# Hybrid decoder layer: host-made channel-first arrays for x, p, weights and vectors, and a per-layer-embedding gate computed channel by channel

## The reference

```
u = rmsnorm(x) * ln_mix;  [x_lru | g_lru | q | k | v] = u @ w_in            # 1024 x 2560
y_lru = rglru(causal_dwconv4(x_lru), gates, lam) * gelu(g_lru)
y_att = moba(rmsnorm(q) * q_gain, rmsnorm(k) * k_gain, v)                   # 2 key blocks of 256, ALiBi
h = x + concat(y_lru, y_att) @ w_out
h = h + (gelu(causal_dwconv3(g_up)) * v_up) @ w_down;  [g_up|v_up] = (rmsnorm(h) * ln_ffn) @ w_up
gate = sigmoid((rmsnorm(h) * ln_ple) @ w_ple_gate)
out = h + gate * (p @ w_ple_proj)
```

## Time and profile before

| | us |
|---|---|
| median of 3 runs | 673.61 (673.38 to 673.63) |
| the profiled execution, its own time | 672.73 |
| its span in the profile | 670.9 |
| PE busy in the span | 660.8 |
| DVE, ACT, POOL busy | 365.1, 288.9, 319.6 |

### The profile page before, as it was taken

The page is one execution under the profiler, slowest core; times in us unless marked ns, Lnnn a source line. Parts: engine busy times, 40 slices in busy tenths (PEclk is TensorE's granted clock), DMA queues, the critical chain, the costliest instruction groups (busy, mean ns, idle before and its releaser), DMA issues.

```text
span 670.9 us, 8848 instructions
## 1 busy us (share of the span) xinstructions
PE 660.8 (98%) x3048; PEld 548.4 (82%) x3048; DVE 365.1 (54%) x522; ACT 288.9 (43%) x435; POOL 319.6 (48%) x234
## 2 busy tenths in 40 slices
PE   7999999999999999999999999999999999999997
PEld 5788888888888888888888888888888888888886
DVE  4687789789867677655555555555522222222033
ACT  4666654656646445333343433333322222224441
POOL 3865443603114648555555555555544444445430
PEclk9999999999999999999999999999999999999999
DMA  8544322210051414333333333333333333332112
GB/s 252 146 126 126 89 84 78 94 33 1 1 158 45 118 57 145 107 94 94 98 97 104 105 96 94 94 94 94 95 94 95 95 99 99 104 102 96 32 43 84
DMA packets 98784, 63.06 MB, mean 94 GB/s; under 512 B 3244, under 2 KB 92232, under 8 KB 98760
## 3 DMA queue, kind: packets, MB, share of 16 engines
q1 hardware_dynamic: 98736, 62.74, 31.6%
q10 hardware_dynamic: 24, 0.01, 0.0%
HBM read 60.64 MB, written 2.10 MB: 94 GB/s over the span
## 4 chain that ended last, share of the span: by engine, by line
PE 93%; DVE 3%; ACT 2%; issue 1%; DMA 1%; SPq 0%; ACTq 0%
PE bank L1055 30%; PE bank L1056 29%; PE bank L1057 29%; ACT prob L536 1%; PE bank L1237 1%; DVE prob L897 1%; DVE prob L885 1%; PE bank L1223 1%; ACT prThi L550 1%; DMA xtok<-in_x 1%; PE bank L1089 1%; PE bank L1350 1%; PE bank L1185 1%; DVE prTlo L933 0%; DVE res L905 0%
## 5 line engine op out<-in xcount | busy, mean ns | idle before, releaser
L335 POOL TENSOR_TENSOR wlo<-raw,whi 128x512 fp32r<-128x512 f32 x108 | 145.2, 1345 | 314.9 <-ACT whi L387 314.8
L387 ACT ACTIVATE whi<-raw 128x1024 fp32r<-128x1024 f32 x107 | 112.9, 1057 | 241.0 <-PE bank L1057 241.0
L1055 PE MATMUL bank<-uhi,whi 128*128 128x512 f32 x446 | 175.1, 393 | 0.2 <-DVE ulo L680 0.2
L1057 PE MATMUL bank<-uhi,wlo 128*128 128x512 f32 x446 | 173.6, 389 | 0.0
L1056 PE MATMUL bank<-ulo,whi 128*128 128x512 f32 x446 | 173.6, 389 | 0.0
L336 POOL TENSOR_TENSOR wlo<-raw,whi 128x512 fp32r<-128x512 f32 x108 | 167.2, 1548 | 0.0
L1055 PEld LDWEIGHTS bank<-uhi,whi 128*128 128x128 f32 x446 | 83.8, 188 | 18.3 <-DVE ulo L680 0.6
L1057 PEld LDWEIGHTS bank<-uhi,wlo 128*128 128x128 f32 x446 | 83.7, 188 | 17.5
L1056 PEld LDWEIGHTS bank<-ulo,whi 128*128 128x128 f32 x446 | 83.7, 188 | 17.4 <-issue 0.5
L988 DVE SCALAR_TENSOR_TENSOR tmp<-tmp,vec 128x511 f32<-128x511 f32 (+1 forms) x48 | 63.4, 1320 | 27.9 <-ACT tmp L599 24.8
L1055 PE MATMUL bank<-acthi,whi 128*128 128x512 f32 x192 | 74.8, 390 | 0.0
(11 more groups left out here) (211 smaller groups left out, 838.4 us busy)
## 6 DMA issues: line engine op xcount, KB each, us to landing
raw<-in_w_up SPq DMA_DIRECT2D x48, 512.0 KB, 3.7
raw<-in_w_down SPq DMA_DIRECT2D x24, 512.0 KB, 3.6
raw<-in_w_in SPq DMA_DIRECT2D x18, 512.0 KB, 3.7
raw<-in_w_out SPq DMA_DIRECT2D x8, 512.0 KB, 3.4
raw<-in_w_ple_gate SPq DMA_DIRECT2D x8, 512.0 KB, 3.7
out<-fin SPq DMA_DIRECT2D x7, 256.0 KB, 2.0
xtok<-in_x SPq DMA_DIRECT2D x4, 256.0 KB, 4.1
xtok<-in_x SPq DMA_DIRECT2D x2, 512.0 KB, 7.4
```

The lines of the kernel that those rows point to most:

```text
L335: nc.gpsimd.tensor_tensor(wlo[s][:, 0:CW // 2], raw[s][:, 0:CW // 2], whi[s][:, 0:CW // 2].bitcast(F32), ALU.subtract)
L387: nc.scalar.activation(whi[s][:, :], raw[s][:, :], ACT.Copy).then_inc(w_hi, 1)
L1055: mm(o, ahi, bhi, start=start, stop=False)
L1057: return mm(o, alo, bhi, start=False, stop=stop)
```

## The change

The host prepares six arrays: `x` as it was, `x_t` (128 x 8 x 512, channels on partitions), `p_t` likewise, `weights` (all chunks one after the other, each 128 rows of 1024 contiguous values, in the order of use), `vectors` (128 x 154, already columns of `vec`) and `gates` (the block-diagonal matrices, zeros included). The output is written as 128 x 8 x 512 and turned by the host. In the kernel:

- `turn_x`, `keep_x` and the vector transposes are gone. `res` is loaded directly, in eight slabs; `norm_x` and `split_u` read it. `xtok` is still loaded, for the sums of squares alone.
- The C_XL weights are cut by input channels instead of output channels. `x_lru(k)` is 12 matmuls, for all four output tiles; for the last two channel tiles the order is by output tile (`x_lru_last`). The row scale moves from the fourth C_XL chunk into the first C_GL chunk.
- The first three weight pieces and ln_mix are issued from ACT's queue; a one-column activation (hb8) follows them.
- The distance table of the attention (POOL iota, cast, select) is made at the start. The softplus chain moves on DVE to a place between `split_u(5)` and `split_u(6)`.
- p's transposes are gone; `pThi` and `pTlo` are made from the loaded `ptok`.
- C_PP and C_PG use the weight as the stationary operand (`project`, `channels`). `turn_h`, `keep_h` and `htok` are gone. The row scale is a full 128x512 array again (`channel_sum_3`: one float32 matmul of ones by `acc`; then DVE, ACT square root of 128x512, DVE reciprocal of 128x512), and multiplies the gate's product on DVE ahead of the sigmoid.

The diff, cut to its core:

```diff
 @@ SP
-            load_x(0)
-            load_head(0, 1).then_inc(head_in[0], 16)
-            load_x(1)
...
-            load_vectors()
+            def load(c, s):
+                if isinstance(c, int) and c < 2 * RING:
+                    sp.wait_ge(half_lo, 2 * (c - RING) + 3)
+                else:
+                    sp.wait_ge(w_lo, c - (2 * RING - 1))
+                sp.dma_start(raw[s][:, :], weights[bass.ds(c * P, P), :]).then_inc(raw_in[s], 16)
+            load_slab(0)
+            load_slab(1)
+            load_slab(2)
+            load_half(2)
+            sp.dma_start(vec[:, KD:NV], vectors[:, KD:NV]).then_inc(vec_in, 16)
+            load_slab(3)
+            load_half(3)
+            load_x(0)
+            load_slab(4)
...
 @@ ACT
+            act.dma_start(vec[:, 0:KD], vectors[:, 0:KD]).then_inc(ln_in, 16)
+            act.dma_start(raw[0][:, 0:2 * P], weights[0:P, 0:2 * P]).then_inc(half_in[0], 16)
+            act.dma_start(raw[0][:, 2 * P:LRU], weights[0:P, 2 * P:LRU]).then_inc(half_in[KD], 16)
+            act.dma_start(raw[0][:, LRU:CW], weights[0:P, LRU:CW]).then_inc(half_in[1], 16)
...
+            nc.scalar.activation(hb8[:, 0:1], ones[:, 0:1], ACT.Copy)
+            act.wait_ge(ln_in, 16)
+            norm_x(0)
+            act.wait_ge(half_hi, 2)
+            for k in range(1, KD):
+                norm_x(k)
+                hi_half(k)
+                if k == 4:
+                    act.wait_ge(sp_step, 1)
+                    nc.scalar.activation(e4, az4, ACT.Exp, scale=-1.0).then_inc(exp_lam, 1)
+                    square_x(0)
...
+            def sigmoid(n, m, c):
+                act.wait_ge(gate_ok, n + 1)
+                nc.scalar.activation(sg[:, m, c], sg[:, m, c], ACT.Sigmoid).then_inc(sig_ok, 1)
...
 @@ DVE
+            for c in range(2, KD - 2):
+                split_u(c, c, V_LN_MIX)
             steps = [1]
...
+            for c in range(KD - 2, KD):
+                split_u(c, c, V_LN_MIX)
...
-                    V.tensor_tensor(sg[:, j, s], sg[:, j, s], pp[:, j, s], ALU.mult).then_inc(mul_ok, 1)
-                    V.tensor_tensor(fin[:, j, s], sg[:, j, s], htok[:, j, s], ALU.add).then_inc(fin_ok, 1)
+            def finish(n, m, c, source):
+                V.tensor_tensor(sg[:, m, c], source, rbc[:, c], ALU.mult).then_inc(gate_ok, 1)
+                dve.wait_ge(pp_ok, m + 1)
+                dve.wait_ge(sig_ok, n + 1)
+                V.tensor_tensor(sg[:, m, c], sg[:, m, c], pp[:, m, c], ALU.mult).then_inc(mul_ok, 1)
+                dve.wait_ge(mul_ok, n + 1)
+                V.tensor_tensor(fin[:, m, c], sg[:, m, c], res[:, m, c], ALU.add).then_inc(fin_ok, 1)
 @@ PE
-            def turn_x(c):
...
+            def x_lru(k):
+                s = k // 2
+                w = [slice((k % 2) * LRU + m * P, (k % 2) * LRU + (m + 1) * P) for m in range(LT)]
+                pe.wait_ge(u_hi, k + 1)
+                pe.wait_ge(half_hi, k + 2 if k else 1)
+                for m in range(LT):
+                    if k == 0 and m == 2:
+                        pe.wait_ge(half_hi, 2)
+                    mm(bank[m][:, :], whi[s][:, w[m]], uhi[:, k, :], start=k == 0, stop=False)
                 pe.wait_ge(u_lo, k + 1)
+                for m in range(LT):
+                    mm(bank[m][:, :], whi[s][:, w[m]], ulo[:, k, :], start=False, stop=False)
+                pe.wait_ge(half_lo, k + 2 if k else 1)
...
+            for m in range(KD - 1):
+                pe.wait_ge(pp_ok, m + 1)
+                channels(C_PG + m, (C_PG + m) % RING, mbank[m][:, :], uhi, ulo, 0, KD, True, True,
+                         before={0: gate_first, 1: channel_sum_3}.get(m))
```

More of the change, by code:

```diff
@@ L317, in _ @@
-            for half in range(2):
-                c = slice(T + half * (T // 2), T + (half + 1) * (T // 2))
-                sp.wait_ge(fin_ok, 2 * TT + half)
-                sp.dma_start(out[(TT - 1) * P:T, c], fin[:, TT - 1, c]).then_inc(out_done, 16)
-            sp.wait_ge(out_done, 16 * (2 * TT + 1))
+            load(C_GL, 0)
+            sp.dma_start(gw[:, :, :, :], gates[:, :, :, :]).then_inc(gw_in, 16)
+            for m in range(1, LT):
+                load(C_GL + m, m)
+            with sp.Fori(2, C_UP // RING) as i:
+                for s in range(RING):
+                    load(i * RING + s, s)
@@ new lines, in x_lru_last, with row_scale @@
+            def x_lru_last(m):
+                for k in (KD - 2, KD - 1):
+                    if m == 0:
+                        pe.wait_ge(u_lo, k + 1)
+                        pe.wait_ge(half_lo, k + 2)
+                    w = slice((k % 2) * LRU + m * P, (k % 2) * LRU + (m + 1) * P)
+                    last = three(bank[m][:, :], whi[3][:, w], wlo[3][:, w], uhi[:, k, :], ulo[:, k, :], False, k == KD - 1)
+                last.then_inc(xl_done if m < LT - 1 else chunk_done, 1)
+            def row_scale():
+                pe.wait_ge(ident_ok, 2)
+                pe.wait_ge(diag_ok, TT)
+                mm(bank[7][:, :], ones[:, :], tmp[:, 3, :], start=True, stop=True).then_inc(bc_done, 1)
@@ L1163, in _ @@
+            for k in range(KD - 2):
+                x_lru(k)
             for m in range(LT):
[L1164 removed]
+                x_lru_last(m)
+            before = {0: lambda k: row_scale() if k == 4 else None, 3: lambda k: pe.wait_ge(rbc_ok, 1) if k == 0 else None}
+            for m in range(LT):
+                channels(C_GL + m, m, bank[4 + m][:, :], uhi, ulo, 0, KD, True, True, before=before.get(m))
             pe.wait_ge(gw_lo, 1)
@@ new lines @@
+    chunks = [chunk(w_in, 2 * s * P, 2, 0, LRU) for s in range(LT)]
+    chunks += [chunk(w_in, 0, KD, LRU + m * P, P) for m in range(LT)]
+    chunks += [chunk(w_in, 2 * s * P, 2, 2 * LRU + t * T, T) for t in range(3) for s in range(4)]
+    chunks += [chunk(w_out, part * LRU, LT, s * 2 * P, 2 * P) for part in range(2) for s in range(4)]
+    chunks += [chunk(w_up, 0, KD, half * FF + f * P, P) for f in range(FT) for half in range(2)]
+    chunks += [chunk(w_down, s * D, KD, m * P, P) for m in range(KD) for s in range(3)]
```

645 lines of the change are left out of this document (228 added, 417 removed).

## The result

| | before | after |
|---|---|---|
| median of the comparison | 673.50 us (672.56 to 673.63, 4 runs) | 667.04 us (666.18 to 667.51, 4 runs) |
| ratio, 95% interval | | 0.9906 [0.9888, 0.9923] |
| the profiled execution, its own time | 672.73 | 666.63 |
| its span | 670.9 | 664.7 |
| PE, DVE, ACT, POOL busy | 660.8, 365.1, 288.9, 319.6 | 652.0, 370.9, 287.1, 318.8 |

The account below looks back on a forecast made before the run. PE was taken to bound the kernel, busy 660.8 of 670.9 us. Terms -4.6 + 0 - 0.9 - 3.5 + 0.5 = -8.5 us from 672.73 gave 664.2; with 0.9 carried over for the median, 665.1 us, range 662.9 to 668.6.

Parts of the forecast that it names:

- rival 1: Head: softplus chain and the splits behind it hold PE; time 668.9 us, chance 0.20 for 666.5 and up.
- The bound of -6.6 on the head: Best case from zero to the first C_GL product: start at 4.6, six slow products, no stall.
- Start at 5.3: Head: PE's first product starts at 5.3 us, at best 4.6, at worst 6.3.
- Slow products, 9.4 with bounds of 6 and 13: Head: first products at the low clock level cost 1.9 us, bounds 1.2 and 2.6.
- Softplus chain, stall of 0.3: Head: 17 DVE steps ahead of `split_u(6)` stall PE at k = 6 by 0.3 us, range 0 to 1.6.
- Its sentence on two SBUF inputs: Rival 1, head: splits now reading two SBUF tiles contend with POOL and can double, 739 to 1502 ns.
- Middle 0: From C_GL to the MLP: no change, at worst +1.5 us if the fourth conv tile is late.
- p -0.9: Ahead of the down projection: removing p's transposes saves 0.9 us.
- gate -3.5: Gate: column sums and transposes gone, one float32 matmul instead; saves 3.5 us.
- Rival 2: Gate's new DVE work shows at the end, up to 2 us more; time 666.5 us, chance 0.07.
- Tail +0.5: After PE's last matmul: one more DVE operation ahead of the sigmoid adds 0.5 us, between +0.4 and +1.2.
- the head's term: From zero to the first C_GL product: -4.6 us, between -6.6 and -0.6.

Follow-up runs that it names:

- c_order: Changed kernel with head loads in order of use on SyncE's queue, ACT issuing ln_mix alone: 664.39 us, ratio 0.9879 to before.
- b_turn8: Changed kernel plus eight unused PE transposes of slab 0 ahead of the first product: 665.13 us, ratio 0.9888 to before.
- a_chain_late: Changed kernel with the softplus chain moved back behind `scale_g(1)` on DVE: 666.11 us, ratio 0.9900 to before.
- a_warm: Changed kernel plus ten unused float32 matmuls of the identity on PE ahead of the first product: 664.77 us, ratio 0.9885 to before.
- a_turns_back: Changed kernel with the removed transposes at p and in the gate put back, outputs unused: 670.70 us, ratio 0.9971 to before.
- b_noscale: Changed kernel without the row scale's product for the last channel tile: 665.63 us, ratio 0.9890 to before.
- a_first: Changed kernel with ACT issuing only the first quarter of weight chunk 0, then ln_mix, the rest on SyncE: 665.24 us, ratio 0.9884 to before.

## Why the prediction was right, and where it was off

The forecast was -8.5 us from the profiled execution, and -6.1 came. The median, 667.04, lies inside the range, but in the part that the prediction had given to rival 1 (from 666.5 on), and rival 1 cost nothing in after; what made it is the head's first two steps, both at their bad end. The bound of -6.6 on the head is a slip: 4.6 + 1.2 + 21.8 + 0.86 = 28.5, which makes it -6.3. By its own steps:

1. *Start at 5.3: wrong, 6.33.* The step counted ACT's issues, the table load and `norm_x(0)`, and these were right to 0.3 us (`uhi` done at 5.0). It gave the landing of the first weight piece one clause ("at worst a weight piece is late and it is 6.3"), and that bound is what happened. Three pieces on ACT's queue and three slabs on SyncE's were under way together: at 4 to 6 us the core moved 309 GB/s, and the first quarter is only 128 KB of it. It took 4.7 us from issue to landing (1.18 to 5.88); c_order, with that piece ahead of everything, has it 2.2 us sooner and starts at 5.26. The Trainium skill, "DMA: Bandwidth & Descriptors", Issuing engines are not separate DMA queues, says that both queues run on the same DMA engines and interleave; the pair of kernels agrees, though c_order moved the piece to the other queue as well. Cost: 1.0 us.

2. *Slow products, 9.4 with bounds of 6 and 13: too few.* Between the first product and the row scale 3.3 us were lost in after (some 0.5 of it at the late second quarter, 2.7 at about 13 slow products), 2.6 to 3.1 in the six other kernels with nothing ahead of the products, where 2.2 were forecast, 0.3 of these for the chain. I let the level rise at the same moment as before, 9.3 us. By the groups of four it rose at about 12.6 in after and between 10.1 and 12.8 in the other six (estimates from where the groups' length falls), so the count was the upper bound of 13, and the slow pitch lasted past 12 us, which the prediction had named as a sign of being wrong. The moment depends on what PE did before: b_turn8 puts transposes back at 4.22, and its level had risen by 7.92, after four slow products. So neither of my readings holds, though the one that counts from before's transposes (13 products) came out nearest. What sets the moment is open. The Trainium skill, "TensorE: Matmul & The Clock Gate", Part 4: PE-mode transpose, says that a transpose does not count as busy for the clock in the way a matmul does; here eight of them brought the loss to 0.8 us where no kernel without them or filling had less than 2.6, and the measurement decides. The trace lists them as MATMUL and does not tell the mode they ran in. Cost: 1.1 us with the next point.

3. *Softplus chain, stall of 0.3: it was 0, in part by luck.* a_chain_late shows no effect. The chain took 5.2 us and not 6.4, but the second split behind it was done at 25.0, where PE at the forecast's pace wanted it at 23.5 + 3 x 0.2267 = 24.2. The 0.8 us between them did not show because PE was late by the points above and wanted it at 26.7. Rival 1 named a real mechanism, which shows 0.46 us in a_warm, where PE is some 2 us earlier. Its sentence on two SBUF inputs held as well: splits of 1.74 us in the head beside POOL's weight parts, against 0.75 before, and not "most escape": the median of the eight in after is 1.78 us. They cost PE nothing but the 0.2 us above.

4. *Middle 0, p -0.9, gate -3.5: right* (2.4 us kept at the down projection, 0.9, 3.65), and a_turns_back gives up 4.47 us of it in its trace, 4.4 to 5.0 in the medians. Rival 2 did not come: the backlog was gone at tile 3, though adds reached 1.67 us there.

5. *Tail +0.5: right*, 0.47 and in b_noscale 0.48. The 0.3 us between DVE's end and the end of the span were not in the sum; no run tells their cause (the stored pieces have other rows).

Head 2.1 and store 0.3 make the 2.4 us of difference. The 0.9 us carried over from the profiled execution to the median came out as 0.4, which leaves 1.9 between 665.1 and 667.04. The mechanism was right outside the head, and the head's term mis-sized: -4.6 forecast, -2.5 measured, inside its bounds. Point 2 has the lesson: before's first transposes ran while the level was low anyway, so taking them out handed the low level to products.

## What to carry to other kernels

Where an engine's first work waits for a load, price the landing of exactly that load by all that is issued with it on every queue, and put the smallest piece that starts PE first. Work that is removed from a cold start may have been nearly free: here the low level was then spent on real products, unless filling took its place. Each repair in the head uncovered the next wait (weight piece, then ln_mix or slab 0, then the split behind the chain), so try them together as well as one by one.

## What the runs showed of the hardware

- A 4 KB load took 3.5 us to land in after, 3.9 in a_first and 3.1 in c_order, with larger ones beside it.
- The clock column reads 1.00 in the head while products pass at 0.425 us, as it did before; in the attention it shows a real fall (0.75, 0.50, 0.90 above), seven products at 0.427 us soon after a wait of 0.54 us. c_order has that wait too and passes at full pitch. What set it off is open.
- Two of the four runs of after have a mean granted clock of 0.996 and are the two longest (667.44, 667.51; 666.63 and 666.18 at 1.000). There is a trace of the 666.63 one alone, so where the clock was lost is open. The fall at 128 us above is in an execution with that same mean, 0.996, and cost 1.6 us, so one such fall would fit.
- A DVE step of four columns takes 0.15 to 0.18 us alone, and up to 1.3 us when a POOL operation is running; then it ends with that operation. It goes the other way as well: in a_first a split that started at 8.85, just before POOL's second weight part (about 8.9), took its usual 0.74 us, and the weight part 1.78 in place of 1.29.
